# Key turns of the first two batch rows, and the first pair's scores, set among the steps of the last prompt tile's output projection

## The reference

```python
attn_o = dsa_prompt(q, k, v, qi, ki, wi)                       # 8 heads, 2 kv heads, top 256 keys of each token
hp = hp + jnp.concatenate([pool_o, attn_o], axis=-1) @ w_out[l]  # output projection and residual
hp = hp + hier_moe(rms_norm(hp, norm_ffn_g[l]), *moe_args)     # router, then 32 experts
...
ksel = gather_paged(cache_k, l, page_table, sel, k, past_len)  # sample rows: 2048 past keys each
vsel = gather_paged(cache_v, l, page_table, sel, v, past_len)
attn_o = dsa_sample(...)                                        # softmax(q k) v over the selected keys
```

## Time and profile before

| | us |
|---|---|
| median of 3 runs (lowest to highest) | 1251.67 (1248.96 to 1254.56) |
| the profiled execution | 1251.29 |
| its span, first to last instruction | 1249.4 |
| PE busy | 1092.7 (87%) |
| DVE busy | 586.6 (47%) |
| ACT busy | 413.7 (33%) |
| mean granted PE clock | 0.936 of full |

### The profile page before, as it was taken

How to read it: one execution, slowest core, us unless ns; L and a number is a source line. 1 busy time by engine, 2 the same in 40 slices (tenths; PEclk the granted TensorE clock), 3 DMA queues, 4 the chain that set the end, 5 groups by cost and what they waited for, 6 DMA issues and landing times.

```text
span 1249.4 us, 16548 instructions
## 1 busy us (share of the span) xinstructions
PE 1092.7 (87%) x6208; PEld 739.4 (59%) x6208; DVE 586.6 (47%) x1285; ACT 413.7 (33%) x976; POOL 191.9 (15%) x253
## 2 busy tenths in 40 slices
PE   4999989899785999999698789679999999999930
PEld 2554523364352677777476455477787887787720
DVE  2224559999997877676531262112211111111128
ACT  1234455567434345555261143211111101111113
POOL 1531215454410000000000110010000000000032
PEclk9999999999886799999699999779999999999975
DMA  6510000010277611111011571379999999999757
GB/s 211 193 45 12 11 22 0 1 34 4 85 186 255 184 51 51 52 52 51 1 52 42 200 305 68 118 270 374 337 334 335 352 329 334 353 330 333 285 173 281
DMA packets 71372, 209.54 MB, mean 168 GB/s; under 512 B 11214, under 2 KB 31774, under 8 KB 61061
## 3 DMA queue, kind: packets, MB, share of 16 engines
q1 hardware_dynamic: 57119, 151.75, 34.5%
q0 software_dynamic: 10448, 44.21, 10.4%
q10 hardware_dynamic: 3742, 12.75, 2.6%
HBM read 171.40 MB, written 37.40 MB: 167 GB/s over the span
## 4 chain that ended last, share of the span: by engine, by line
PE 78%; DVE 12%; ACT 3%; DMA 3%; issue 3%; POOL 1%; SPq 0%; POOLq 0%; ACTq 0%; DVEq 0%; PEldq 0%
PE ps L1451 18%; PE ps L1457 9%; PE ps L1296 7%; PE ps L1085 5%; PE ps L1101 5%; PE ps L1112 5%; PE ps L1040 3%; PE ps L1073 3%; PE ps L1243 3%; PE ps L1444 2%; PE ps L1254 2%; DVE mem L1996 2%; PE ps L1266 2%; ACT mem L1527 2%; DVE mem L2333 2%
## 5 line engine op out<-in xcount | busy, mean ns | idle before, releaser
L1527 ACT ACTIVATE mem<-ps 128x512 f32<-128x512 f32 (+10 forms) x376 | 173.0, 497 | 348.5 <-PE ps L1254 72.9
L1451 PEld LDWEIGHTS ps<-mem 128*128 128x128 f32 x2048 | 235.9, 193 | 16.8 <-issue 16.8
L1451 PE MATMUL ps<-mem 128*128 128x96 f32 x2048 | 235.4, 276 | 0.8 <-DVE mem L2400 0.8
L1996 DVE TENSOR_SCALAR_CACHE_REDUCE mem<-mem 128x768 bf16<-128x768 f32 (+2 forms) x134 | 166.5, 1282 | 0.0
L1296 PE MATMUL ps<-mem 128*128 128x256 f32 (+1 forms) x544 | 126.5, 385 | 5.8 <-ACT mem L1527 2.8
L1457 PE MATMUL ps<-mem 128*96 128x512 f32 x256 | 117.6, 602 | 2.4 <-DVE mem L2392 2.3
L1296 PEld LDWEIGHTS ps<-mem 128*128 128x128 f32 (+1 forms) x544 | 100.0, 189 | 23.0 <-ACT mem L1527 3.7
L2392 DVE TENSOR_TENSOR mem<-mem,ps 128x192 f32<-128x192 f32 x32 | 11.4, 356 | 213.3 <-ACT mem L1867 213.3
L1867 ACT ACTIVATE mem<-ps 128x192 f32<-128x192 f32 x32 | 10.6, 333 | 264.2 <-PE ps L1451 264.2
L977 POOL DMA_INDIRECT mem<-xn_rows,mem x32 | 29.0, 907 | 371.7 <-PE ps L1444 316.0
L2333 DVE CUSTOM_DVE_ANT_0 mem<-ps,mem 128x128 f32<-128x128 f32 (+7 forms) x64 | 48.2, 753 | 53.1 <-PE ps L1243 53.1
(11 more groups left out here) (289 smaller groups left out, 1414.7 us busy)
## 6 DMA issues: line engine op xcount, KB each, us to landing
mem<-in_expert_w_gate SPq DMA_DIRECT2D x32, 1024.0 KB
mem<-in_expert_w_up SPq DMA_DIRECT2D x32, 1024.0 KB
mem<-in_expert_w_down SPq DMA_DIRECT2D x32, 1024.0 KB
expert_rows<-mem ACTq DMA_DIRECT2D x32, 384.0 KB
expert_rows<-mem SPq DMA_DIRECT2D x2, 4608.0 KB, 29.6
mem<-in_x_prompt SPq DMA_DIRECT2D x16, 512.0 KB, 4.2
mem<-in_w_in SPq DMA_DIRECT2D x3, 2048.0 KB, 10.9
h_rows<-mem SPq DMA_DIRECT2D x8, 512.0 KB, 2.7
```

The costliest lines, as they stand in the source:

```text
L1451: ins = mm(ps[:, 2 + s, j * CAP:(j + 1) * CAP], wgu[w][:, j // 2, k, (j % 2) * P:(j % 2 + 1) * P], xgT[:, s, k, :], start=(k == 0), stop=( ...
L1527: return fn(out, in_, ACT.Copy, scale=scale)
L1996: v.tensor_scalar(bufs[a % 3][0:R, 0:w], sc, mid[:, a:a + 1], None, ALU.is_ge, ALU.add, accum_out=cnt[:, a:a + 1]).then_inc(step, 1)
```

## The change

Eight new steps `("K", b, c)` (turn chunk c of the keys of batch row b, b = 0 and 1) and one step `("SC", 0)` (scores of the first pair) are put between the tail steps that follow the last attention. `keys` and `keep_keys` take a list of chunks. PE's first K step waits until bank 5 is copied out and until the last prompt outputs are kept (bank 6); the copies on DVE and ACT wait for the last `V`, since `KTs` lies on `Sm`. `SC` waits for banks 0 to 4 and the mask. The wait for `Vnew_in` stays behind the border. In POOL's list the gather of keys 2 moves from behind the border (after values 1) to before it, behind a wait for the last prompt scores to be masked, as its buffer lies on the masks.

```diff
-        tasks += [("OP", i - 1, 3), ("SQ", i - 1), ("OT", i), ("OP", i, 0), ("NM", i - 1), ("OP", i, 1), ("XR", i - 1, 0),
-                  ("OP", i, 2), ("XR", i - 1, 1), ("OP", i, 3), ("LG", i - 1), ("SQ", i), ("OP", NT, 0), ("NM", i), ("OP", NT, 1),
-                  ("XR", i, 0), ("OP", NT, 2), ("XR", i, 1), ("OP", NT, 3), ("LG", i)]
+        tasks += [("OP", i - 1, 3), ("SQ", i - 1), ("OT", i), ("K", 0, 0), ("OP", i, 0), ("K", 0, 1), ("NM", i - 1), ("OP", i, 1), ("K", 0, 2),
+                  ("XR", i - 1, 0), ("OP", i, 2), ("K", 0, 3), ("XR", i - 1, 1), ("OP", i, 3), ("K", 1, 0), ("LG", i - 1), ("SQ", i),
+                  ("OP", NT, 0), ("K", 1, 1), ("NM", i), ("OP", NT, 1), ("K", 1, 2), ("XR", i, 0), ("OP", NT, 2), ("K", 1, 3),
+                  ("XR", i, 1), ("OP", NT, 3), ("SC", 0), ("LG", i)]
...
             pool.memset(zrow, 0.0).then_inc(zrow_ready, 1)
+            pool.wait_ge(emptied["2bA"], use["2b"]["A"] * NKV)
+            past(Kin, ck_rows, 2, K_in)
             pool.wait_ge(prompts_done, 3)
             tiles_out(pool, h_out, NT)
             tiles_out(pool, x2_out, NT)
             past(Vin, cv_rows, 1, V_in)
-            past(Kin, ck_rows, 2, K_in)
...
+            for t in tasks:
+                if t[0] == "K":
+                    if t[1:] == (0, 0):
+                        pe.wait_ge(emptied["2bPT1"], use["2b"]["PT1"])
+                        pe.wait_ge(o_kept, NT)
+                    keys(t[1], (t[2],))
+                elif t[0] == "SC":
+                    pe.wait_ge(emptied["2bA"], use["2b"]["A"] * NKV)
+                    pe.wait_ge(emptied["2bPT0"], use["2b", "PT0", ("OP", NT, 5)])
+                    pe.wait_ge(smask_ready, 1)
+                    scores_of(t[1])
...
-            keys(0)
-            keys(1)
-            scores_of(0)
             keys(2)
             keys(3)
...
             for t in tasks_elsewhere:                      # ACT
                 kind, i = t[0], t[1]
-                if kind == "S":
+                if kind == "K":
+                    if t[2] >= 2:
+                        act.wait_ge(av_done, NT * PAIRS)
+                        keep_keys(t[1], (t[2],))
+                elif kind == "SC":
+                    continue
+                elif kind == "S":
...
-            keep_keys(0)
-            keep_keys(1)
             exps(0)
...
             for t in tasks_elsewhere:                      # DVE
                 kind, i = t[0], t[1]
-                if kind == "S":
+                if kind == "K":
+                    if t[2] < 2:
+                        dve.wait_ge(av_done, NT * PAIRS)
+                        keep_keys(t[1], (t[2],))
+                elif kind == "SC":
+                    continue
+                elif kind == "S":
...
-            keep_keys(0)
-            keep_keys(1)
             for p in range(NPAIR):
                 take(dve, "2c", "SS", p)
```

More of the change, by code:

```diff
@@ L502, in program @@
                     npt += 1
-            elif t[0] not in ("SQ", "NM", "V"):
+            elif t[0] not in ("SQ", "NM", "V", "K", "SC"):
                 orderB.append((part_of(t), t))
@@ L1317, in tail, with keys @@
                 ins.then_inc(filled["2bM"], 1)
[L1319 to L1340, removed]
+            def keys(b, chunks=range(4)):
                 s = b % 3
                 pe.wait_ge(K_in[s], 16 * (b // 3 + 1))
-                for c in range(4):
+                for c in chunks:
                     part = tk_use["k", b, c]
@@ L1363, in scores_of @@
                 ins.then_inc(filled["2cSS"], 1)
+            for t in tasks:
[9 more added lines that the diff above has]
+                    scores_of(t[1])
+                elif t[0] == "S":
+                    q_k(t[1], t[2])
+                elif t[0] == "T":
+                    p_turn(*t[1:])
+                elif t[0] == "V":
+                    p_v(t[1], t[2])
+                else:
+                    tail(t)
+            pe.wait_ge(emptied["2bM"], use["2b", "M", ("OP", NT, 4)])
+            pe.drain().then_inc(prompts_done, 1)
+            pe.wait_ge(prompts_done, 3)
+            pe.wait_ge(Vnew_in, 16)
             def probs_turn(p):
@@ L1765, in tail, with keep_keys @@
                     fn(r1[0:r, 3:4], r1[0:r, 1:2], ACT.Exp).then_inc(gexp_ready, 1)
+            def keep_keys(b, chunks=(2, 3)):
+                for c in chunks:
+                    part = tk_use["k", b, c]
+                    take(act, "2c", f"TK{part}", ("k", b, c))
+                    copy(KTs[:, b % 2, 512 * c:512 * (c + 1)], ps[:, 5 + part, :]).then_inc(emptied[f"2cTK{part}"], 1)
             for t in tasks_elsewhere:
                 kind, i = t[0], t[1]
-                if kind == "S":
+                if kind == "K":
[5 more added lines that the diff above has]
+                elif kind == "S":
                     h, w, u = t[2], P * (i + 1), i * PAIRS + t[2]
@@ L1799, in _ @@
             flat = ps[:, :, :].rearrange("p b n -> p (b n)")
[L1801 to L1805, removed]
             def exps(p):
@@ L2319, in some_pieces, with keep_keys @@
                     over.append(next(waiting, "all done"))
+            def keep_keys(b, chunks=(0, 1)):
+                for c in chunks:
+                    part = tk_use["k", b, c]
+                    take(dve, "2c", f"TK{part}", ("k", b, c))
+                    v.tensor_copy(KTs[:, b % 2, 512 * c:512 * (c + 1)], ps[:, 5 + part, :]).then_inc(emptied[f"2cTK{part}"], 1)
             for t in tasks_elsewhere:
                 kind, i = t[0], t[1]
-                if kind == "S":
+                if kind == "K":
[5 more added lines that the diff above has]
+                elif kind == "S":
                     h, w, u = t[2], P * (i + 1), i * PAIRS + t[2]
```

## The result

The changed kernel takes 1255.92 us (median; 1254.24 to 1256.73), the one before 1251.67 on the same chip: a ratio of 1.0035, 95% interval 1.0018 to 1.0051. The forecast was 1256.0. The profiled execution has a span of 1253.7 (1249.4 before). The tail steps, `OP`(6,3) first, begin at 662.69 in it and at 661.96 before; the 0.7 us between them arise at the start of the program, in the first loads.

A forecast was written before the change was run, and what follows sets the result against it. Bound by waits between PE steps, then the chain or transfer gating keys 3: border +6.0, landing +14.5, less 18.3, gives +2.3; clock +2.4 makes +4.7 on 1251.29, so 1256.0 us; 8 in 10 for 1250.0 to 1261.0.

The forecast's parts named there:

- Key turns: Tail steps: eight added K steps mostly fit PE's idle gaps and cost 0.7 us, bounds 0 to 5.3.
- third rival: Tail steps: the K steps don't fit the gaps and cost 5.3 us; 1260.6 us in all, chance 0.10.
- Scores: Tail steps: SC takes 5.8 us of PE with one 0.51 us wait to hide in, so +5.3 us.
- The border: End of LG of tile 7, forecast to move from 704.07 to 710.1, +6.0 us.
- Landing of keys 3: Start of 2c: the gather of keys 3, beside expert weights, lands 14.5 us after LG's end, at 724.6.
- first rival: Start of 2c: the gather of keys 3 is not late; 1246.9 us, or 1245.0 if before 716.0; chance 0.10.
- The statement that the early landing of keys 2 is worth nothing: Start of 2c: keys 2 landing early gains nothing, as its chunks 2 and 3 wait for DVE's maximum and copies.
- The maximum, exponential and ACT's copy take what they took: Start of 2c: the chain from DVE's maximum to keys 3 stays 5.2 us long.
- The clock: Behind the wait for keys 3: 6 us at low clock slow the 33 transposes, +2.4 us (1.2 to 3.7).
- second rival: Behind the wait for keys 3: low clock outlasts the 33 turns; +9.2 us, 1260.5 us, chance 0.15.
- I take every shift at the end of 2c as a shift of the end: Expert stage: it starts when 2c ends and passes any shift on unchanged to the kernel's end.
- The forecast's own range: Whole kernel: 1252.9 (no clock price, K steps free) to 1258.6 us; the forecast had chance 0.65.

The follow-up runs named there:

- e3: The changed kernel with the scores of pair 0 put back behind the border, the key turns staying among the tail steps; 1248.48 us, 0.9983 of the kernel before.
- e1: The changed kernel with the gather of keys 3 also issued ahead of the border; 1245.01 us, 0.9945 of the kernel before.
- e2: The changed kernel with expert 0's weights issued only after keys 3 are turned; 1247.53 us, 0.9969 of the kernel before.
- e4: The changed kernel with the gather of keys 2 put back behind the border, after values 1; 1255.23 us, 1.0030 of the kernel before.
- e5: The changed kernel with gathers of values 1, keys 3 and 4 and the exponential's table load ahead of the border; 1244.16 us, 0.9954 of the kernel before.
- e9: e5 with 14 filler transposes between the halves of keys 2 and 4 behind it; 1243.57 us, 0.9938 of the kernel before.
- e7: e5 with the scores of pair 0 put back behind the border; 1247.31 us, 0.9957 of the kernel before.
- e8: The changed kernel with 50 filler transposes on PE between keys 2 and keys 3; 1255.03 us, 1.0041 of the kernel before.

## Why the prediction was right

The mechanism was the one forecast: the border moves later by the scores, and the wait for keys 3 takes the place of the work that was moved. Step by step:

- **Key turns**, forecast +0.7, measured 0.2 (e3's `LG` against before's). The gaps hide them, and the third rival falls.
- **Scores**, forecast +5.3, measured 5.0 (47.3 less 42.3). The border moved by 5.2 instead of 6.0.
- **Landing of keys 3**, forecast 14.5 behind `LG`, measured 15.4 and 15.1 to the start of their turns. With the border: keys 3 start 2.4 us later from OP than before (2.3 forecast); the two errors cancel. e1 and e2 show the cause, not only the wait: the first takes the gather out of the queue, the second the weights. The first rival (a gather that lands in 5.9 us) needed the weights out of the way; with them out it took 8.0.
- **The statement that the early landing of keys 2 is worth nothing** was wrong. For keys 2 it holds, but the early gather also leaves a place in the queue, and keys 3 move up: 2.2 us at the scores of pair 1 (e4). My own sum used just that place, and the sentence contradicted it.
- **"The maximum, exponential and ACT's copy take what they took"** was off by 1.3 us. In the kernel before, the exponential's table was loaded at 712.01, while ACT waited for the maximum; after the change the load stands behind that wait (713.02). It cost nothing here, hidden by the DMA; it is the 1.3 us between e1 and e5 at keys 3 (7.0 and 5.7).
- **The clock** is the term that was mis-sized: forecast +2.4 (6 us low), measured +1.0: from the start of keys 3 to the scores of pair 1 it is 6.67 us against 5.71, and the clock returned 3.6 us after work resumed, near the lower end of my bounds. The second rival falls; the clock came back among transposes, as in the trace before. The cause that I gave, the long wait, isn't borne out: the clock had fallen at 712, just as PE began a wait of 1.92 us between the halves of keys 2, and in e1, without the long wait, it fell there as well and the same work took 7.09 us. With transposes in the 1.92 us wait (e9) it took 5.71. So a price of the right sign came from the start of 2c; that the wait for keys 3 adds to it isn't shown.
- **"I take every shift at the end of 2c as a shift of the end"** held for this pair of kernels and not in general. The scores of pair 1 are 3.35 us late and the end 3.5 (591.0 against 587.5 from OP), as both kernels have the same 10.2 us of low clock behind 770. In e4, e5 and e7 the way to expert 0 is 0.9 to 4.0 us shorter. The forecast had this by luck: I never asked whether a shift would change a later stretch of low clock.

The forecast's own range has a slip: its upper end, 1258.6, is the +6.9 of unhidden key turns on the median, its lower end is +1.6 on the profiled execution, and neither holds a price of the clock. The result lies well inside either way.

The traces give +3.5 and, in the second one, +3.0; the medians +4.2 against +4.7 forecast. The rest between traces and medians is within what single executions scatter.

## What to carry to other kernels

Work moved ahead of a barrier is free only while it fits into waits, and it is worth only what the next late thing allows: before moving compute, list the transfers that are issued behind the barrier and move those first. Here eight turns cost 0.2 us and one gather's place was worth 8 us at its landmark. A list's position decides a gather's landing twice over, by its issue and by what else fills the engines: keys 3 landed after 5.8 us ahead of the border (e1), 8.0 behind it without the weights (e2) and 13.6 beside them. And small edits should be judged at landmarks near them as well as by the total, since a later stretch of low clock can give or take 2 to 4 us for reasons unrelated to the edit.

## What the runs showed of the hardware that was not expected

The low clock between 770 and 795 lasted from 0 to 10.2 us in these nearly equal programs, and its length repeated in both programs that were traced twice. That each program has a fixed length isn't shown: over the whole kernel the mean clock differs between executions of one program (0.927 to 0.933 in the second series of the changed kernel). At the start of 2c the clock fell as a wait of 1.9 us began (changed kernel, e1), and stayed up where 14 transposes filled it (e9). Filling PE's waits raised the clock in some places (expert 0's products 7.36 instead of 9.71 us) and not to the end of the wait in e8, where the filler was too short. A table load of ACT runs ahead of a wait in one order of instructions and behind it in another; its 1.28 us can so enter a chain without any edit to the step that it belongs to.
